# One core: third branch projection and output projection run token tile by token tile, the merge and its transposes placed between the tiles

## What is computed

```
y_a = o_a @ w_branch[:FOX_W]
y_b = o_b @ w_branch[FOX_W:FOX_W + SB_W]
y_c = o_c @ w_branch[FOX_W + SB_W:]
gates = jax.nn.sigmoid(bgates).reshape(B, S, N_BRANCH, D_MODEL)
merged = gates[:, :, 0] * y_a + gates[:, :, 1] * y_b + gates[:, :, 2] * y_c
return merged @ w_o
```

## Time and profile before

| | |
|---|---|
| runs | 1502.47, 1504.43 (median), 1507.83 us |
| the profiled execution | 1508.85 us, of which the span from first to last instruction is 1507.1 us |
| mean granted TensorE clock | 0.948 |
| TensorE matmul busy | 1381.2 us, 92% of the span |
| VectorE busy | 1016.0 us, 67% |
| ScalarE busy | 655.1 us, 43% |
| GpSimd busy | 132.4 us, 9% |
| DMA | 295.19 MB, mean 196 GB/s |

### The profile page before, as it was taken

How to read it: one execution, slowest core, us unless ns; L and a number is a source line. 1 busy time by engine, 2 the same in 40 slices (tenths; PEclk the granted TensorE clock), 3 DMA queues, 4 the chain that set the end, 5 groups by cost and what they waited for, 6 DMA issues and landing times.

```text
span 1507.1 us, 17718 instructions
## 1 busy us (share of the span) xinstructions
PE 1381.2 (92%) x6960; PEld 1162.8 (77%) x6960; DVE 1016.0 (67%) x1249; ACT 655.1 (43%) x904; POOL 132.4 (9%) x234
## 2 busy tenths in 40 slices
PE   3799987998999987999979999989899998799996
PEld 2688866887899775888868888869878987688885
DVE  6677765685776757787566786468578666656545
ACT  0544422555743424444324444336665342344441
POOL 4000111000000101010010011010000000000000
PEclk9999998899999988999979999969989998899998
DMA  9587883565554534787736878436546453355651
GB/s 336 166 286 262 286 303 98 182 196 168 159 176 146 193 102 132 260 286 283 267 106 217 283 262 328 140 116 209 183 136 196 129 180 112 112 186 179 222 187 64
DMA packets 193188, 295.19 MB, mean 196 GB/s; under 512 B 13577, under 2 KB 157233, under 8 KB 193105
## 3 DMA queue, kind: packets, MB, share of 16 engines
q1 hardware_dynamic: 172336, 220.43, 44.3%
q0 software_dynamic: 20768, 73.63, 14.4%
HBM read 292.97 MB, written 1.05 MB: 195 GB/s over the span
## 4 chain that ended last, share of the span: by engine, by line
PE 77%; DVE 10%; issue 6%; DMA 3%; ACT 3%; POOL 1%; SPq 0%; DVEq 0%; ACTq 0%; POOLq 0%
PE pg L849 65%; DMA aw<-in_w_ada_dram 2%; PE pt L1145 1%; DVE acc L1425 1%; PE pt L874 1%; PE pt L1157 1%; PE pt L813 1%; PE pt L1155 1%; DVE acc L1345 1%; DVE stats L1502 1%; DVE x L1496 1%; DVE lnw L1493 1%; ACT whi L495 1%; DMA pro<-in_w_ada_dram 1%; DVE wlo L1394 1%
## 5 line engine op out<-in xcount | busy, mean ns | idle before, releaser
L1394 DVE TENSOR_TENSOR wlo<-wraw,whi 128x1024 fp32r<-128x1024 f32 (+1 forms) x408 | 487.4, 1202 | 366.3 <-ACT whi L495 365.3
L495 ACT ACTIVATE whi<-wraw 128x1024 fp32r<-128x1024 f32 (+1 forms) x408 | 423.7, 1041 | 517.8 <-PE pg L849 509.1
L849 PE MATMUL pg<-whi,hhi 128*128 128x512 f32 (+1 forms) x1088 | 443.6, 408 | 15.7 <-DVE wlo L1394 8.1
L849 PE MATMUL pg<-whi,hlo 128*128 128x512 f32 (+1 forms) x1088 | 430.4, 396 | 0.0
L849 PE MATMUL pg<-wlo,hhi 128*128 128x512 f32 (+1 forms) x1088 | 430.0, 395 | 0.0
L849 PEld LDWEIGHTS pg<-whi,hhi 128*128 128x128 f32 x1088 | 212.6, 195 | 61.5 <-issue 12.7
L849 PEld LDWEIGHTS pg<-whi,hlo 128*128 128x128 f32 x1088 | 212.1, 195 | 45.1
L849 PEld LDWEIGHTS pg<-wlo,hhi 128*128 128x128 f32 x1088 | 212.8, 196 | 42.2 <-issue 1.9
L1425 DVE SCALAR_TENSOR_TENSOR acc<-aw,sc,acc 128x1024 f32<-128x1024 f32 x128 | 163.9, 1280 | 25.3 <-DMA aw<-in_w_ada_dram 22.0
L849 PE MATMUL pg<-whi,athi 128*128 128x512 f32 x352 | 141.5, 402 | 7.1 <-DVE wlo L1394 6.4
L379 POOL DMA_DIRECT2D aw<-in_w_ada_dram x128 | 68.1, 532 | 852.7 <-DVE acc L1425 845.8
(11 more groups left out here) (308 smaller groups left out, 1265.6 us busy)
## 6 DMA issues: line engine op xcount, KB each, us to landing
wraw<-in_ffn_w_up_dram SPq DMA_DIRECT2D x176, 512.0 KB, 4.8
aw<-in_w_ada_dram POOLq DMA_DIRECT2D x128, 512.0 KB, 5.1
wraw<-in_w_in_dram SPq DMA_DIRECT2D x104, 512.0 KB, 4.7
wraw<-in_ffn_w_down_dram SPq DMA_DIRECT2D x88, 512.0 KB, 4.5
pro<-in_w_ada_dram SPq DMA_DIRECT2D x8, 1024.0 KB, 14.5
wraw<-in_w_branch_dram SPq DMA_DIRECT2D x16, 512.0 KB, 4.4
wraw<-in_w_o_dram SPq DMA_DIRECT2D x16, 512.0 KB, 3.9
lnbc<-in_ln_g_dram POOLq DMA_DIRECT2D x6, 512.0 KB, 5.7
```

Source lines behind the costliest of these rows:

```text
L495: act.activation(whi[:, n % 4, 0:size], wraw[:, q, o:o + size], ACT.Copy).then_inc(S["w_hi"], 1)
L849: ins = pe.matmul(out_ap, a[i], b[j], start=first and n == 0, stop=last and n == 2, skip_group_check=group)
L1394: dve.tensor_tensor(lo, a, whi[:, n % 4, 0:size].bitcast(F32), ALU.subtract).then_inc(S["w_lo"], 1)
```

## The change

TensorE's halves 60 to 66 are taken out of the loop over halves and put in a new function, `last_branch`, which runs halves 60 to 63 for tile 0, then the same for tile 1, then halves 64 to 66 for tile 0, then for tile 1. `merged_T(0)` stands after half 61 of tile 1 and `merged_T(1)` after half 65 of tile 0. VectorE's `gated` and `merge` take a tile each; for the third branch, tile 0 is multiplied and added in slot 60 and tile 1 in slot 62, behind `merged_lo(0)`. ScalarE's `merged_hi(0)` moves from slot 63 to slot 62. `mod_columns` moves from behind half 66 to behind half 67. No instruction is added or removed.

```
                        if q == 55:
                             o_sq(1)
+                        if q == 62:
+                            merged_hi(0)
                         if q == 63:
-                            merged_hi(0)
                             merged_hi(1)
...
-                def merged_T():
-                    for t in range(NT):
-                        pe.wait_ge(S["merged"], at("merged", 2 * t + 2))
...
+                def merged_T(t):
+                    pe.wait_ge(S["merged"], at("merged", 2 * t + 2))
...
-                    if q == 63:
-                        merged_T()
-                    if q == 66:
+                    if q == 67:
                         pe.wait_ge(S["m_lo"], at("m_lo", 2))
...
+                def last_branch():
+
+                    for q in range(60, 64):
+                        rows_half(q // 2, q % 2, (0,))
+                    for q in range(60, 64):
+                        rows_half(q // 2, q % 2, (1,))
+                        if q == 61:
+                            merged_T(0)
+                    for q in range(64, 67):
+                        rows_half(q // 2, q % 2, (0,))
+                        if q == 65:
+                            merged_T(1)
+                    for q in range(64, 67):
+                        rows_half(q // 2, q % 2, (1,))
+
...
-                            if not 3 <= q < 2 * MIX_U - 3:
+                            if q == 60:
+                                last_branch()
+                            if not 3 <= q < 2 * MIX_U - 3 or 60 <= q < 67:
                                 continue
...
                             if b == 2:
-                                dve.wait_ge(S["merged1"], at("merged1", 4))
+                            dve.wait_ge(S["merged1"], at("merged1", 2 * t + n + 1))
...
+                        if q in (57, 59):
+                            for t in range(NT):
+                                gated((q - 57) // 2, t)
+                        if q == 60:
+                            for t in range(NT):
+                                merge(1, t)
+                            gated(2, 0)
+                            merge(2, 0)
+                        if q == 62:
+                            merged_lo(0)
+                            gated(2, 1)
+                            merge(2, 1)
                         if q == 63:
-                            merged_lo(0)
                             merged_lo(1)
```

More of the change, by code:

```diff
@@ L1208, in o_T @@
                     ins.then_inc(S["o_T"], 1)
-                def merged_T():
-                    for t in range(NT):
-                        pe.wait_ge(S["merged"], at("merged", 2 * t + 2))
[L1213 to L1216, removed]
+                def merged_T(t):
+                    pe.wait_ge(S["merged"], at("merged", 2 * t + 2))
+                    for c in range(KD):
+                        ins = pe.transpose(pt[:, 2 * t + c // 4, (c % 4) * P:(c % 4 + 1) * P],
+                                           merged[:, t, c * P:(c + 1) * P], ident[:, :])
+                    ins.then_inc(S["merged_T"], 1)
                 def slot_work(q):
@@ L1759, in c_lo @@
                                       hhi[:, 4:8, :].bitcast(F32), ALU.subtract).then_inc(S["o_lo"], 1)
[L1761 to L1783, removed]
-                                dve.wait_ge(S["merged1"], at("merged1", 4))
-                            dve.tensor_tensor(m, m, g, ALU.add).then_inc(S["merged" if b == 2 else "merged1"], 1)
+                def gated(b, t):
+                    for n in (0, 1):
+                        if (t, n) == (1, 1):
+                            dve.wait_ge(S["w_used"], at("w_used", 2 * (U_M + BR0 + (1, 2, 4)[b])))
+                        else:
+                            dve.wait_ge(S["yb_mm"], at("yb_mm", 3 * b + 2 * t + n + 1))
+                        g = gates[:, t, b * D + n * 512:b * D + (n + 1) * 512]
+                        if b == 0:
+                            dve.wait_ge(S["mix_ev"], at("mix_ev", MIX_CH))
+                            dve.wait_ge(S["zq_mm"], at("zq_mm", 1))
+                        dve.tensor_tensor(merged[:, t, n * 512:(n + 1) * 512] if b == 0 else g,
+                                          pg[:, 2 * t + n, :], g, ALU.mult).then_inc(S["y_ev"], 1)
@@ new lines, in merge @@
+                def merge(b, t):
+                    for n in (0, 1):
+                        g = gates[:, t, b * D + n * 512:b * D + (n + 1) * 512]
+                        m = merged[:, t, n * 512:(n + 1) * 512]
+                        dve.wait_ge(S["y_ev"], at("y_ev", 4 * b + 2 * t + n + 1))
+                        if b == 2:
+                            dve.wait_ge(S["merged1"], at("merged1", 2 * t + n + 1))
+                        dve.tensor_tensor(m, m, g, ALU.add).then_inc(S["merged" if b == 2 else "merged1"], 1)
```

## The result

The changed kernel takes 1491.62 us (median of 6 runs, 1489.57 to 1494.18) against 1503.61 for the kernel before (6 runs, 1500.87 to 1507.83): a ratio of 0.9915, 95% interval 0.9896 to 0.9934, or 10 to 16 us less. The forecast was 1492.8.

What follows compares the result with a forecast made beforehand. TensorE was taken as the bound. Per layer, 9.05 us lost less 1.76 of transposes and 1.5 of waits saves 5.79; both layers save 11.6, taking 1504.43 to 1492.8 us, range 1488.5 to 1498.5.

Steps and rivals of the forecast that it cites:

- two sets of transposes: Eight TensorE transposes for each tile's merged result, still paid inside the matmul stream: 0.88 us a set, 1.76 per layer.
- the wait at half 64 of tile 0: TensorE waits for tile 0's low part from VectorE before half 64's first matmul: 0.25 us.
- the wait at tile 1: TensorE waits after half 66 of tile 0 for tile 1's splitting, in place of the old wait: 1.25 us.
- no fall: TensorE's clock stays full through the new stretch from half 60 to mod_columns; chance 0.52, 1492.8 us.
- the row at 512.10: Profile row: after eight transposes and a wait of 1.12 us, TensorE's next matmuls ran with the clock full.
- The old gap: TensorE's stretch without matmuls before half 64, for merge, transposes and splitting; with slow matmuls after it, 9.05 us per layer.
- The reading of the Trainium skill: If transposes cannot keep the full clock, it falls in both layers and the gain is 8.4 us.
- rival 1: The clock falls at the new wait in one layer or both: gain 9.95 or 8.4 us, 1494.5 or 1496.1; chance 0.27.
- The margins of 0.6, 0.4: Microseconds by which VectorE's merges of tile 0 and tile 1 would be ready before TensorE's transposes.
- Rival 2: VectorE becomes the bound of the stretch, costing 1 to 2 us more per layer: 1495 to 1497 us; chance 0.14.
- Later stages: Sign of being wrong altogether: stages behind, dependent on DMA and VectorE's ada work, take up the 5.8 us as waiting.
- The DMA queue: Possible cause of no measurable gain (chance 0.05): weights given back later make a DMA late; judged twice over hidden.

Runs made afterwards that it cites:

- branch_only: The changed kernel, but halves 64 to 66 run both tiles in each half, with merged_T(1) before half 64; 1501.01 us, ratio 0.996 to the kernel before.
- proj_only: The changed kernel, but halves 60 to 63 run both tiles in each half, both transpose sets before half 64; 1499.15 us, ratio 0.9958 to the kernel before.
- late_T: The changed kernel with merged_T(1) one half later, behind half 66 of tile 0; 1504.03 us, ratio 0.9992 to the kernel before.
- four_halves: The changed kernel with half 67 drawn into the tile by tile part; 1491.2 us, ratio 0.9916 to the kernel before.
- mod_split: The changed kernel with mod_columns cut in two, behind halves 67 and 68; 1490.69 us, ratio 0.9919 to the kernel before.
- all: The changed kernel with four_halves, mod_split and the same cut of mod_columns in three FFN stages; 1485.4 us, ratio 0.9869 to the kernel before.

## Why the prediction was right

**The sum.** 5.79 per layer was forecast, and D is 5.58 and 5.66 shorter. Its terms, forecast and measured in the first layer: two sets of transposes 2 x 0.88 and 2 x 0.88; the wait at half 64 of tile 0 0.25 and 0.24; the wait at tile 1 1.25 and 1.24. What is missing is small: from half 60 to the end of half 66 is 22.72, where 540.75 - 518.22 = 22.53 was worked out, and of the 0.19 between them 0.16 is the first step behind each of the two waits, 0.31 instead of 0.23, which I had counted as a plain step. That D carries over nearly whole rests on the clock: it fell nowhere between half 60 and `mod_columns`, and the stretch behind `mod_columns` stayed as slow as it had been.

**The cover.** That the gain comes from matmuls of the other tile is shown by branch_only and proj_only (part of the gain each, with the waits at the places worked out) and by late_T, where taking 1.38 us of cover away lengthened the wait by as much.

**The clock.** I took no fall, on the row at 512.10, and it did not fall, in 6 layers of 6. late_T shows how near that was: a wait of 2.6 us behind eight transposes brings the clock down in 4 layers of 6 and leaves it full in 2. The old gap brought it down always, in all four layers of the two profiles that still have it. The reading of the Trainium skill that I set against this (TensorE: Matmul & The Clock Gate, Part 4, PE-mode transpose) does not hold here as a rule for keeping the clock: eight transposes and, six matmuls later, a wait of 1.24 left it full.

One price was too small: a fall was put at 1.61 per layer. The old one had cost 0.6 more, in its transposes, and one in late_T costs 3.2, as `mod_columns` and the matmuls behind it are then slow for longer. If a fall at the wait of 1.24 cost as much (an estimate; none was seen there), two of them would have left a gain of 2 x (5.6 - 3.2) = 4.8 us and a time of 1499.6, above the range that I gave. So rival 1 was underpriced (its 9.95 for one fall is also 9.97 by its own terms), and that did not matter only because it did not come.

**VectorE and ScalarE.** The margins of 0.6, 0.4 (0.49 by its own figures) and 0.2 came out as 0.64, 0.60 and 0.25, the last from 528.40 + 1.22 to the first matmul of half 66 at 529.87. Rival 2 needed more than these to be used up. In late_T and four_halves one sees both sides: putting the transposes behind half 66 exposes the low part, and one more low part ahead of `merged_lo(1)` costs nothing.

**Later stages** gave nothing back: D is counted up to the layer norm, and both layers delivered. The DMA queue played no part that the trace shows: in this stretch both waits of TensorE end with VectorE's `hlo`, and ScalarE's waits before the high parts of weights are ended by TensorE.

**The size of the whole.** It is 11.24 us in the two D, against 12.0 between the medians and 17.0 between the two spans. That 1491.62 lies only 1.2 from the forecast of 1492.8 is partly luck, as executions of one kernel differ by 5 to 7 us here; the 11.24 beside 11.6 is the comparison that counts. A reader with the spans alone would put 5.8 us too much down to the change.

## What to carry to other kernels

When a step needs a complete result of everything before it, let another part of the work run its last matmuls first, and count what that covers: the merge, the transposes and the splitting each need their own stretch of matmuls, and the last one here was one half too short. Look at the clock in and behind each gap, as a gap's price includes slow work there, and at tiny matmuls in one long piece: cutting `mod_columns` in two gave 1.5 us per layer, as much as closing the last wait (1.3). Measure an edit between two fixed instructions in the trace when the whole time scatters by more than the effect.

## What the runs showed of the hardware that I had not expected

TensorE is shown busy for all of `mod_columns` (3.50 of 3.50 us, 32 matmuls of one column), and still the clock was at the lower level behind it, at once or after a few steps, in 20 of 20 mixer stages: both layers of the ten profiles that have it uncut there. In two pieces of 1.7 us with 2.7 us of wide matmuls between, it stayed full in 4 of 4 (mod_split and all), and in 2 of the 3 FFN stages of all. Uncut in the FFNs it was followed by slow steps in 11 of 11 profiles in the first stage, 8 of 11 in the second and 2 of 11 in the third; what makes that difference is open.
